# A one-core encoder trunk: the order of constant, weight and memory loads, 16 constant products ahead of the data, and another way to memory's norm column

## The reference

```
h     = rmsnorm(x, g_mix);      proj = h @ w_in
mixed = gated short convolution (layer 0) or stick-breaking attention (layer 1) of proj
mem_kv = rmsnorm(mem, g_mem) @ w_mem_kv          # 256 memory tokens, keys and values, 4 heads of 128
k, v  = split(mem_kv);  q = last 512 columns of proj
p     = softmax(rmsnorm(q, g_q) @ rmsnorm(k, g_k).T * 128 ** -0.5)
x     = x + concat(mixed, p @ v) @ w_out
h     = rmsnorm(x, g_ffn)
x     = x + (silu(h @ w_gate) * (h @ w_up)) @ w_ffn_out      # d_ff 2816
```

## Time and profile before

| | us |
|---|---|
| median of 3 runs | 2652.38 (2651.53 to 2652.42) |
| span of the profiled execution, first to last instruction | 2646.9 |
| TensorE matmul busy | 2562.6 (97%) |
| VectorE busy | 1784.0 (67%) |
| ScalarE busy | 1204.7 (46%) |
| GpSimd busy | 719.9 (27%) |
| mean granted TensorE clock | 0.989 |

### The profile page before, as it was taken

How to read it: one execution, slowest core, us unless ns; L and a number is a source line. 1 busy time by engine, 2 the same in 40 slices (tenths; PEclk the granted TensorE clock), 3 DMA queues, 4 the chain that set the end, 5 groups by cost and what they waited for, 6 DMA issues and landing times.

```text
span 2646.9 us, 34791 instructions
## 1 busy us (share of the span) xinstructions
PE 2562.6 (97%) x12320; PEld 2130.7 (80%) x12320; DVE 1784.0 (67%) x2247; ACT 1204.7 (46%) x2027; POOL 719.9 (27%) x523
## 2 busy tenths in 40 slices
PE   8899999999999999999999999998899999999999
PEld 8688887888888887887878888886788888887887
DVE  6566666167756577775677777777648665758667
ACT  6463333144434443335666666665424443444332
POOL 2502220102323222233033333333120322222322
PEclk9899999999999999999999999999999999999999
DMA  6412225213433456534111111112321342437634
GB/s 208 152 40 72 78 90 191 80 63 116 146 116 119 151 177 246 217 147 159 49 37 33 33 32 32 32 32 107 125 101 53 139 161 77 152 133 273 236 145 157
DMA packets 85923, 311.39 MB, mean 118 GB/s; under 512 B 10417, under 2 KB 10417, under 8 KB 73137
## 3 DMA queue, kind: packets, MB, share of 16 engines
q1 hardware_dynamic: 74304, 261.17, 28.0%
q0 software_dynamic: 11216, 42.47, 4.5%
q10 hardware_dynamic: 288, 6.29, 0.6%
HBM read 220.24 MB, written 89.65 MB: 117 GB/s over the span
## 4 chain that ended last, share of the span: by engine, by line
PE 79%; DVE 7%; issue 7%; ACT 4%; POOL 1%; DMA 1%; SPq 0%; ACTq 0%; DVEq 0%; POOLq 0%
PE ps L2334 25%; PE ps L2336 24%; PE ps L2335 24%; PE ps L2646 1%; POOL sig L968 1%; DVE aT_lo L1955 1%; PE ps L2662 1%; DVE tile_lo L2203 1%; DVE w_lo L1584 1%; DVE keep L1913 1%; ACT keep L1313 1%; PE ps L2663 1%; PE ps L2595 1%; ACT sq L1325 1%; PE ps L2596 1%
## 5 line engine op out<-in xcount | busy, mean ns | idle before, releaser
L2334 PE MATMUL ps<-tile_hi,g_hi 128*128 128x512 f32 x1680 | 661.3, 394 | 7.7 <-DVE tile_lo L2203 5.2
L2336 PE MATMUL ps<-tile_hi,g_lo 128*128 128x512 f32 x1680 | 658.3, 392 | 0.0
L2335 PE MATMUL ps<-tile_lo,g_hi 128*128 128x512 f32 x1680 | 654.7, 390 | 0.0
L2334 PE MATMUL ps<-xg_hi,w_hi 128*128 128x512 f32 x1024 | 412.6, 403 | 4.5 <-DVE xg_lo L1783 3.3
L2336 PE MATMUL ps<-xg_hi,w_lo 128*128 128x512 f32 x1024 | 402.6, 393 | 0.0
L2335 PE MATMUL ps<-xg_lo,w_hi 128*128 128x512 f32 x1024 | 402.1, 393 | 0.0
L2334 PEld LDWEIGHTS ps<-tile_hi,g_hi 128*128 128x128 f32 x1680 | 316.2, 188 | 76.1 <-issue 5.5
L2336 PEld LDWEIGHTS ps<-tile_hi,g_lo 128*128 128x128 f32 x1680 | 316.0, 188 | 71.5
L2335 PEld LDWEIGHTS ps<-tile_lo,g_hi 128*128 128x128 f32 x1680 | 316.3, 188 | 69.0
L1482 ACT ACTIVATE g_hi<-quads 128x512 fp32r<-128x512 f32 x310 | 194.9, 629 | 359.0 <-PE ps L2336 328.8
L2132 DVE TENSOR_TENSOR g_lo<-quads,g_hi 128x512 fp32r<-128x512 f32 x310 | 281.4, 908 | 107.1 <-ACT g_hi L1482 103.1
(11 more groups left out here) (277 smaller groups left out, 4338.4 us busy)
## 6 DMA issues: line engine op xcount, KB each, us to landing
quads<-wpack SPq DMA_DIRECT2D x62, 1024.0 KB, 5.9
raw<-wpack SPq DMA_DIRECT2D x88, 512.0 KB, 3.3
d_split<-x SPq DMA_DIRECT2D x116, 256.0 KB, 6.3
tile_lo<-d_tile SPq DMA_DIRECT2D x30, 512.0 KB, 7.5
d_tile<-R SPq DMA_DIRECT2D x46, 256.0 KB, 6.4
d_tile<-x SPq DMA_DIRECT2D x46, 256.0 KB, 6.1
cquads<-wpack SPq DMA_DIRECT2D x10, 1024.0 KB, 4.8
tile_hi<-d_split SPq DMA_DIRECT2D x10, 1024.0 KB, 8.5
```

What stands on the lines that cost most here:

```text
L2334: pe.matmul(out, whi, mhi, start=start, stop=False, skip_group_check=chained)
L2335: pe.matmul(out, whi, mlo, start=False, stop=False, skip_group_check=chained)
L2336: return pe.matmul(out, wlo, mhi, start=False, stop=stop, skip_group_check=chained)
```

## The change

- The three constant loads move from the head of SyncE's list to the head of ScalarE's. SyncE begins with the first weight unit and memory.
- TensorE makes 16 products of two constant tiles, 128 columns each into bank 7, as soon as the constants are made; nobody reads them. Only then comes the first key product. The wait on `consts_made` stands ahead of them now.
- The 16 one-column products, their root and their reciprocal are gone. Instead the reciprocal row `mr`, which is the same on all partitions, is transposed in two blocks of 128 by TensorE after the fourth key product, and VectorE copies one column of each block into `mcol`, ahead of its work on the value units. ScalarE's first values and TensorE's second value group wait for `mcol_ready`; the second group uses bank 5, in which the transposes stood.
- ScalarE's wait for both reciprocals is gone, TensorE's wait for both roots is now one for `mr`.

```diff
@@ SyncE @@
-            for name, src in vectors:
-                dst = {"gain": gain, "taps": taps, "g_heads": g_heads}[name]
-                sp.dma_start(dst[:], src).then_inc(consts_in, 16)
             for s in range(WSLOTS):
                 sp.dma_start(raw[s][:], slabs(KB * s, KB)).then_inc(raw_landed[s], 16)
@@ ScalarE @@
+            for name, src in vectors:
+                dst = {"gain": gain, "taps": taps, "g_heads": g_heads}[name]
+                act.dma_start(dst[:], src).then_inc(consts_in, 16)
             act.wait_ge(ident_steps, 4)
...
             act.activation(mrt[:], ps[:, 4, 0:NMEM], ACT.Sqrt, bias=eps[:, 0:1]).then_inc(mroot_ready, 1)
-            act.activation(mcol_t[:], ps[:, 5, 0:2], ACT.Sqrt, bias=eps[:, 0:1]).then_inc(mroot_ready, 1)
             for m in range(KB):
                 act.activation(mg_hi[1][:, m, :], mem[:, m, :], ACT.Copy, scale=gain[:, 1, 1, m:m + 1]
                                ).then_inc(mg_hi_ready, 1)
-            act.wait_ge(mr_ready, 2)
...
                     if i > 0:
                         act.wait_ge(kv_stored, 64 * i)
+                    elif g == 0:
+                        act.wait_ge(mcol_ready, 1)
@@ VectorE @@
-            dve.wait_ge(mroot_ready, 2)
+            dve.wait_ge(mroot_ready, 1)
             dve.reciprocal(mr[:], mrt[:]).then_inc(mr_ready, 1)
-            dve.reciprocal(mcol[:], mcol_t[:]).then_inc(mr_ready, 1)
             memory_lo(1)
-            dve.wait_ge(mr_ready, 2)
+            dve.wait_ge(mr_ready, 1)
...
+                if i == 0:
+                    dve.wait_ge(mcol_full, 1)
+                    dve.tensor_copy(mcol[:], ps[:, 5, 0:2 * P].rearrange("p (b c) -> p b c", b=2)[:, :, 0]).then_inc(mcol_ready, 1)
+                    dve.wait_ge(mcol_ready, 1)
                 for g in range(2):
@@ TensorE @@
+            pe.wait_ge(consts_made, 4)
+            for _ in range(WARMUP):          # WARMUP = 16
+                pe.matmul(ps[:, 7, 0:P], mean_head[:], mean_all[:], start=True, stop=True)
             memory_keys(0, 0)
-            pe.wait_ge(consts_made, 4)
             pe.wait_ge(msq_ready, 1)
             for k in range(KB):
-                pe.matmul(ps[:, 4, 0:NMEM], mean_all[:], msq[:, k, :], start=(k == 0), stop=(k == KB - 1))
-            for mb in range(2):
-                for k in range(KB):
-                    last = pe.matmul(ps[:, 5, mb:mb + 1], msq[:, k, mb * P:(mb + 1) * P], mean_all[:, 0:1],
-                                     start=(k == 0), stop=(k == KB - 1))
+                last = pe.matmul(ps[:, 4, 0:NMEM], mean_all[:], msq[:, k, :], start=(k == 0), stop=(k == KB - 1))
             last.then_inc(mstat_full, 1)
...
                 if i == 0:
-                    pe.wait_ge(mroot_ready, 2)
+                    pe.wait_ge(mr_ready, 1)
+                    for mb in range(2):
+                        last = pe.transpose(ps[:, 5, mb * P:(mb + 1) * P], mr[:, mb * P:(mb + 1) * P], ident[:])
+                    last.then_inc(mcol_full, 1)
                 for g in range(2):
+                    if i == 0 and g == 1:
+                        pe.wait_ge(mcol_ready, 1)
```

More of the change, by code:

```diff
@@ L48 @@
 MASKED = -1.0e30
+WARMUP = 16
 A_UNITS = 2 * MHEADS
@@ L179, in trunk @@
         mcol = place("mcol", [P, 2], F32)
-        mcol_t = place("mcol_t", [P, 2], F32)
         rq_v = place("rq_v", [P, KB], F32)
@@ L341, in trunk @@
         mr_ready = sem("mr_ready")
+        mcol_full = sem("mcol_full")
+        mcol_ready = sem("mcol_ready")
         gqk_ready = sem("gqk_ready")
```

## The result

The changed kernel takes 2661.35 us (median of 6 runs, 2658.90 to 2664.09), the kernel before 2651.79 (6 runs): ratio 1.0037, with a 95% interval of 1.0026 to 1.0049 (intervals below are 95% too). It is 9.6 us slower; forecast was 0.6 us faster, with a range up to 2654.0.

What follows compares the result with a forecast made beforehand. The prediction took TensorE to bound the body and x's landing the edited opening. A 1.0 us gain at VectorE's row less 0.4 given back made 0.6: 2652.4 - 0.6 = 2651.8 us, range 2648.6 to 2654.0.

Steps and rivals of the forecast that it cites:

- Everything behind 66 us is the same work and shifts.: Whole kernel after the opening: unchanged work that only starts earlier by the opening's gain, 0.6 us.
- Constants to ScalarE's queue, s = 1.2: Start of the opening: s, the shift of every step that follows from memory landing, is 1.2 us earlier.
- the front doesn't move: Rival, opening: constants on the other queue delay the weights, s = 0, x lands at T = 36.5; 2653.0 us, chance 0.10.
- Sixteen constant products: TensorE, opening: they absorb the slow-clock time, end at 10.5 to 12; statistics start 0.9 us earlier.
- Norm column by transposes: Opening: 32 one-column records, 4.13 us, leave the path; transposes cost nothing while x is late, else 0.4 us.
- the 0.9 that was to come from an earlier `msq`: TensorE, opening: statistics start at 13.9 instead of 14.8 us, bounded by `msq` ending at 13.4.
- But then x is late.: x's load, opening: earlier weight loads share the DMA and push x by 3.0 us, landing at T = 35.3.
- the 36.3 that I had named as a sign of being wrong: x's load, opening: x landing after 36.3 us, or before 33, would show the forecast wrong.
- What is given back: Layer 1's first key product: slow clock throughout after longer idling, 5.1 us instead of 4.7, a loss of 0.4.
- the formula 36.3 - T: VectorE's row after x: gain is 36.3 minus T, x's landing time; 1.0 us at T = 35.3.
- slower: Rival, layer 1's first two memory keys: x lands at 36.9 and TensorE stays at 1.2 GHz; 2655.7 us, chance 0.08.
- The 5.5 us around the span: Outside the profiled span: 2652.38 less 2646.9 leaves 5.5 us, taken to stay unchanged.

Runs made afterwards that it cites:

- e2: Kernel before with only `mcol_t` placed behind all other tiles, so the tiles behind it lie 32 bytes lower: 2657.77 us, ratio 1.0025 to the kernel before.
- e9: Changed kernel with old addresses, constants back on SyncE and x issued behind the second high weight unit instead of the third: 2650.79 us, ratio 0.9996 to before.
- e1: Changed kernel with an unused 32-byte tile in place of the deleted `mcol_t`, restoring the old addresses: 2653.62 us, ratio 1.0004 to the kernel before.
- e11: Changed kernel, whole edit, with the same tile layout as e10: 2641.86 us, ratio 0.9967 to the kernel before.
- e10: Kernel before with small tiles behind everything and FFN and convolution moving operands at multiples of 512 bytes: 2638.54 us, ratio 0.9954 to the kernel before.

## Why the prediction was wrong, point by point

- **"Everything behind 66 us is the same work and shifts."** This step failed. The instructions are the same; the addresses of their operands are not. I costed the deleted root and reciprocal of `mcol_t` and never the deleted tile, though the full diff has the line and the layout's cursor is in the code. It is worth 6.6 us (e2; 4.0 to 9.0), most of the 9.6. None of the rivals had it.
- **Constants to ScalarE's queue, s = 1.2.** Failed: s = -0.2. The first weights did move by 1.25 us, and memory's first half, which ended the wait before, was there at 7.1 (issued at 1.4, 5.7 us to landing). But beside weights and memory the constants took 4.0 to 6.8 us to land instead of 1.6 to 1.7, and the first instruction on memory needs them. The rival "the front doesn't move", at 0.10, had s = 0 and T = 36.5, but for another reason: it had the weights delayed, and they were not.
- **Sixteen constant products.** Right: 5.79 us against my 6.5, over at 10.0, and the first key product, at 10.50, runs with its matmuls 0.12 us apart, where they were 0.21 apart before. It was not even held up, as memory's low part came late, with the constants. No run leaves these products out by themselves.
- **Norm column by transposes.** Right: 4.1 us off TensorE's path. The statistics came 4.0 us earlier instead of 5.0; the 0.9 that was to come from an earlier `msq` hung on s. The key products behind them start their matmuls 0.12 us apart, at granted clock 1.00 from 21.1 to 27.9 us, where it was 0.50.
- **"But then x is late."** Right, and the largest term of the opening: x was pushed back, its last half taking 20.0 us to land instead of 16.6. I had put the push at 3.0, and it was 3.4. It was issued 0.1 us later instead of 1.2 earlier, so my formula gives 33.5 + 0.1 + 3.0 = 36.6; it landed at 37.1, past the 36.3 that I had named as a sign of being wrong. e9 confirms that x holds the opening. The even split of the queues held while both had work: 0.79 to 0.80 MB from 29 to 33 us.
- **What is given back.** Right: layer 1's first key product ran at granted clock 0.61 over its stretch and the next `w_hi` started 5.0 us behind its first matmul (4.7 before, 5.1 forecast). With T = 37.1 the formula 36.3 - T less this 0.3 gives -1.1, and the `w_hi` is 1.2 us later than before (53.62 against 52.44). The rival "slower" had x this late, but its low clock in two products came for most of the first alone.
- **The 5.5 us around the span.** Wrong by 3.8 us, though without effect on a difference; the profiled execution was a short one.

The opening alone, by these steps corrected, gives +1 us at 108 us, as measured; e1, with the layout restored, is at 1.0004 with an interval of about 2.5 us to either side. Of the 9.6 us, 6.6 are shown to be the layout, by a measurement that leaves 4.0 to 9.0, and 1.0 is seen in the opening. The remaining 2 are smaller than these intervals and stay open. e11 against e10 hints that the edit's own cost may be more than the opening's microsecond, and no run settles that.

## What to carry to other kernels

Deleting or adding a tile in a hand-made layout is an edit of every tile behind it: compare the addresses first, and when a uniform loop far from the edit changes its pace without any wait, look there. Lay the moving operands of the busiest matmuls at multiples of 512 bytes from the arena's start, as e10 does, and put the small tiles behind them. And when work ahead of a big load is made faster, ask what it will issue into that load; here 5 us of saved key work turned into 1 MB more of weights moved beside x.

## What the runs showed of the hardware that I had not expected

Two matmul streams with the same shapes, the same clock and no wait differ by up to 3% with the address of the moving operand: in the FFN's products 227 ns from start to start at a multiple of 512 bytes, 229 at a remainder of 320, and 233 at 288 and 352, 233 to 234 at 384. The mean is the same in the two FFN layers of a run to within 0.1 ns. With one of the two moving operands off, in the convolution, the order is another: a product takes 2.80 us at 320 and 2.75 at 384. A transfer of 2 KB (`g_heads`) took 1.7 us to land when it stood ahead of the weights in SyncE's queue, and 6.8 us when it was issued on ScalarE's queue at 1.88 us while SyncE issued 2.5 MB between 0.95 and 3.2.
